# Two slots for product weights and two for condition units in the ring of the convolution part

## The chip, the cores and the metric

One core of one Trainium2 chip. The metric is the device time of the kernel in microseconds (us); less is better. TensorE, VectorE, ScalarE and GpSimd are called PE, DVE, ACT and POOL; SP is the queue that issues most of the loads. PEld is PE's weight load.

## The reference, cut to what matters

One step of a decoder layer on 512 prompt rows and 8 x 8 sample rows (576 columns in all), all in float32. What the change touches is the convolution branch and the condition product that runs beside it:

```python
m = jnp.dot(jax.nn.silu(c), w_ada) + b_ada          # 9 condition rows, 2048 x 12288
h = _rmsnorm(x, norm1) * (1 + sc1) + sh1
z = jnp.dot(h, w_in)                                # 2048 x 4688, za and zg 1024 wide each
a = za * jax.nn.sigmoid(zg)
y = _dwconv_valid(a_hist, w_dw_a, b_dw_a)           # 31 taps along the sequence, 1024 channels
conv_o = jax.nn.silu(_group_layernorm(y, gn_g, gn_b))   # 8 groups of 128 channels
```

The last 30 rows of `a` (and the sample's) are outputs too. After this come the attention part, the merge and a gated MLP.

## The kernel before, in words

The program is written by hand for each engine, with semaphores between them; the order of each engine's instructions is the order of the code. All big products are float32 by three passes: ACT copies a weight tile `raw` to `whi` (`hi`, L735), POOL subtracts, `wlo = raw - whi` in four instructions of 128x256 (`lo`, L663), and PE multiplies `whi` by the high part of the operand, `whi` by its low part, and `wlo` by the high part (`unit`, L1074). `raw` has four slots of 512 KB, `whi` and `wlo` two each.

The convolution part is `mix(i)` for i = 0 to 7, one group of 128 channels each. Two kinds of tiles pass through `raw`:

- four halves of product weights (two of `zg`, two of `za`), which go through ACT and POOL and are then one `part` of 48 matmuls on PE;
- eight condition units (256 x 512 of `w_ada`), which PE reads straight from `raw` (`ada_unit`, L1108), without ACT and POOL. Two of them stand behind each part: a pair.

In the code before, units are numbered 0 to 11 within `mix(i)`: product weights are k = 0, 3, 6, 9, the others condition units, and `Tally.slot` gives slot k mod 4 (plus the base). So each load takes the slot of the unit four places earlier. A load by SP waits until that slot is read: `taken(n)` waits for POOL's subtraction of product weight n (s_lo), `multiplied(n)` for PE's condition unit n (s_au). The loads of product weights k = 6, 9 and 0 of the next group stand in slots of condition units, and wait for these:

```python
ada_done(1)
half(u, 6, 0, win, i * 128 + C_ZA)
...
ada_done(3)
half(u, 9, 1, win, i * 128 + C_ZA)
```

PE in `mix(i)`: part 0, `ada_sum`, `group_var(i-2)` (L1269), pair 0, part 1, `last_rows(i-1)` (L1297), `group_root(i-2)` (L1276), pair 1, part 2, pair 2, `state_in(i)` (L1305), part 3, pair 3, `group_center(i-1)` (L1262). Parts are counted 0 to 3 here in both kernels.

ACT in `mix(i)`: copy of weight 1, `ada_sums`, `squares`, `silu_conv`, copy of weight 2, `ada_out`, `root_var(i-2)` (L813, two small square roots and a table load), copy of weight 3, the sigmoid of zg (`sg`, L851), `last_rows(i-1)` (copies to `cvs`, L825, L826), copy of the next group's weight 0, `state_in`.

DVE in `mix(i)`: the gated product (`hist`, L1830), which waits for part 3 and the sigmoid; then 31 taps in two chains (`yb` L1860, `ye` L1863), with between them the sample rows (`prod` L1844, its reduction L1847), the reciprocal of the roots (L1812) after tap 13, `norm_group` (L1817) after tap 25, the sum of the two chains (L1866), and one step of the top-k of the scores (`take_prompt`, L1795, L1800). DVE's `mix(i)` runs while PE is in `mix(i+1)`.

POOL: the four subtractions of the group, then two output DMAs (L677).

The next part (`U_QKV`) uses the ring of four for product weights alone; there the DVE work of `mix(7)` and eight more top-k steps come first.

Of the kernel before, what the change touches and what calls it, by code (L numbers as in the profile page):

```python
# [114 lines left out]
class Tally:  # L115
# [5 lines left out]
    def __init__(self, base, i=0, per=0):  # L121
        self.base, self.i, self.per = base, i, per
        self.whole = ADA1 if base < U_QKV else ADA1 + ADA2 if base < U_ADB else ADA1 + ADA2 + ADA3
        self.whole_per = 8 if U_MIX <= base < U_QKV else 0

    def slot(self, k, n):
        assert self.per % n == 0
        return (self.base + k) % n

    def turn(self, k, n):  # L130

        return (self.base + k) // n + self.i * (self.per // n)

    def index(self, k):
        if self.whole_per:
            assert k % 3 == 0
            return self.base - self.whole + k // 3 + self.i * (self.per - self.whole_per)
        return self.base - self.whole + k + self.i * self.per

# [35 lines left out]
def layer_program(nc, x_prompt, x_sample, cache_k, cache_v, cache_kidx, state_conv, state_ffn, page_table,  # L175
# [7 lines left out]
    with ctx:  # L183
# [244 lines left out]
        def _(sp):  # L428
            def taken(n):

                sp.wait_ge(s_lo, n + 1)

            def multiplied(n):

                sp.wait_ge(s_au, n + 1)
# [61 lines left out]
            def ada_part(u, k, m, nb):  # L497
                weight(u, k, rows(w_ada[0, m * 256:m * 256 + 256, nb * 512:nb * 512 + 512], 2), 512)

            def mix(i):  # L500
                u = Tally(U_MIX, i, 12)
                ada_done = lambda m: multiplied(ADA1 + 8 * i + m)
                if i == 0:
                    before = [lambda k=k: taken(u.index(0) - 4 + k) for k in range(4)]
                else:
                    before = [lambda: ada_done(-3), lambda: taken(u.index(0) - 1), lambda: ada_done(-2), lambda: ada_done(-1)]
                before[0]()
                half(u, 0, 0, win, i * 128 + C_ZG)
                before[1]()
                ada_part(u, 1, 0, i + 8)  # L510
                before[2]()
                ada_part(u, 2, 1, i + 8)
                before[3]()
                half(u, 3, 1, win, i * 128 + C_ZG)
                w(sp, s_stt, i)
                sp.dma_start(stN[:, :, :], state_conv[0].rearrange("b r c -> (b r) c")[:, i * 128:i * 128 + 128]
                             .rearrange("(h p) c -> p h c", h=2)).then_inc(s_stn, 16)
# [6 lines left out]
                taken(u.index(3))  # L524
                ada_part(u, 7, 4, i + 8)
                ada_done(2)
                ada_part(u, 8, 5, i + 8)
                ada_done(3)
                half(u, 9, 1, win, i * 128 + C_ZA)
                taken(u.index(6))  # L530
                ada_part(u, 10, 6, i + 8)
                ada_done(4)
                ada_part(u, 11, 7, i + 8)
            w(sp, s_scD, 1)
            for i in range(8):
                mix(i)

# [13 lines left out]
            n = ADA1 + ADA2  # L551
            before = [lambda: multiplied(n - 3), lambda: taken(u.index(0) - 1), lambda: multiplied(n - 2), lambda: multiplied(n - 1)]
            for c in range(4):
# [101 lines left out]
        def _(pool):  # L655
# [23 lines left out]
            for i in range(8):  # L679
                for k in (0, 3, 6, 9):  # L680
                    lo(Tally(U_MIX, i, 12), k, 1)
                if i:
                    conv_rows(i - 1)
# [18 lines left out]
        def _(act):  # L702
# [131 lines left out]
            def mix(i):  # L834
                u = Tally(U_MIX, i, 12)
                hi(u, 3)
                if i:
# [3 lines left out]
                if i >= 3:  # L841
                    silu_conv(i - 3)
                hi(u, 6)
# [213 lines left out]
        def _(pe):  # L1057
# [250 lines left out]
            def mix(i):  # L1308
# [6 lines left out]
                if i >= 2:  # L1315
                    group_var(i - 2)
                ada_unit(u, 1, 0)
                ada_unit(u, 1, 1)
                part(u, 3, 0, 1)
                if i:  # L1320
# [3 lines left out]
                for m in (2, 3):  # L1324
                    ada_unit(u, 2, m)
                w(pe, s_a, i)
                part(u, 6, 1, 0)
                for m in (4, 5):
                    ada_unit(u, 3, m)
                state_in(i)  # L1330
                part(u, 9, 1, 1)
                for m in (6, 7):
# [305 lines left out]
        def _(dve):  # L1638
# [186 lines left out]
            def mix(i):  # L1825
                u = Tally(U_MIX, i, 12)
                dve.wait_ge(s_used, u.index(9) + 3)
                dve.wait_ge(s_sg, i + 1)
# [344 lines left out]
```

## Time and profile before

| | us |
|---|---|
| median of 3 runs | 3378.21 (3371.06 to 3380.23) |
| the profiled execution, its time | 3379.13 |
| its span in the trace | 3377.5 |
| convolution part, first to last `hist` (seven intervals) | 474.55 to 784.75 |

The trace is of one execution. The starts of `hist` (L1830) on DVE mark the groups: 474.55, 522.69, 566.47, 609.58, 651.83, 696.00, 739.24 and 784.75 us. Every rate below is read between two of these.

### The profile page before, as it was taken

Reading aid. Unit: us, or ns where it says so; the run is one execution under the profiler, and the core shown is the slowest. Engines: PE = TensorE matmul, PEld = TensorE weight load, DVE = VectorE, ACT = ScalarE, POOL = GpSimd, SP = SyncE. Lnnn points to the kernel's source line nnn. Section 1 sums busy time; section 2 is a strip of 40 time slices with the busy share of each in tenths; the row PEclk is TensorE's granted clock in tenths of the full one; section 3 lists DMA queues with packets and bytes.
Section 4 is the critical chain, followed back from the end, with each engine's and each line's share of the span. In section 5 each row is a group of like instructions: output and inputs, shape, how many; then the busy total and the mean of one; then the engine's idle time right before and its main releaser. Section 6 shows DMA issues by size and latency. Waiting matters only on the chain.

```text
span 3377.5 us, 56831 instructions
## 1 busy us (share of the span) xinstructions
PE 3108.6 (92%) x21589; PEld 2767.3 (82%) x21592; DVE 1358.1 (40%) x2796; ACT 899.0 (27%) x1640; POOL 1220.4 (36%) x1694
## 2 busy tenths in 40 slices
PE   6698969899997788799799999999999999999998
PEld 3196357778973444599699999999999999999998
DVE  1524246778877744300523232332323232332322
ACT  2212312323212221211232323232332323232323
POOL 0042333334330023144244444444444444444443
PEclk9897889999998777799699999999999999999999
DMA  7821144553237455423122222322222222222223
GB/s 244 261 73 34 38 140 142 154 154 102 70 110 245 144 152 154 121 75 89 32 82 87 84 82 86 86 82 83 88 83 82 86 85 83 83 86 85 82 84 94
DMA packets 448315, 356.83 MB, mean 106 GB/s; under 512 B 27785, under 2 KB 391973, under 8 KB 446885
## 3 DMA queue, kind: packets, MB, share of 16 engines
q1 hardware_dynamic: 437282, 327.85, 32.6%
q0 software_dynamic: 8704, 19.27, 2.0%
q10 hardware_dynamic: 2075, 6.34, 0.6%
q8 instruction: 158, 2.59, 0.3%
q14 instruction: 96, 0.78, 0.1%
HBM read 346.15 MB, written 7.96 MB: 105 GB/s over the span
## 4 chain that ended last, share of the span: by engine, by line
PE 69%; issue 14%; DVE 5%; POOL 4%; DMA 4%; ACT 2%; SPq 1%; POOLq 0%; DVEq 0%; ACTq 0%
PE ps L1074 58%; POOL wlo L663 4%; DMA raw<-in_w_in 3%; PE ps L1108 1%; PE ps L1214 1%; PE ps L1485 1%; PE ps L1246 1%; PE ps L1472 1%; PE ps L1276 1%; PE ps L1238 1%; DMA raw<-in_w_ada 1%; ACT whi L735 1%; PE ps L1269 1%; PE ps L1435 0%; DVE mx L1964 0%
## 5 line engine op out<-in xcount | busy, mean ns | idle before, releaser
L663 POOL TENSOR_TENSOR wlo<-raw,whi 128x256 fp32r<-128x256 f32 x1480 | 1108.0, 779 | 1715.6 <-ACT whi L735 1715.6
L1074 PE MATMUL ps<-XH,whi 128*128 128x288 f32 (+1 forms) x4512 | 991.0, 301 | 71.8 <-POOL wlo L663 52.5
L1074 PE MATMUL ps<-XH,wlo 128*128 128x288 f32 (+1 forms) x4512 | 977.0, 298 | 0.0
L1074 PE MATMUL ps<-XL,whi 128*128 128x288 f32 (+1 forms) x4512 | 973.1, 297 | 0.0
L735 ACT ACTIVATE whi<-raw 128x1024 fp32r<-128x1024 f32 x370 | 391.2, 1058 | 1744.8 <-PE ps L1074 1463.3
L1074 PEld LDWEIGHTS ps<-XH,whi 128*128 128x128 f32 (+1 forms) x4512 | 734.5, 191 | 100.4 <-issue 47.6
L1074 PEld LDWEIGHTS ps<-XL,whi 128*128 128x128 f32 (+1 forms) x4512 | 734.5, 191 | 0.0
L1074 PEld LDWEIGHTS ps<-XH,wlo 128*128 128x128 f32 (+1 forms) x4512 | 732.0, 191 | 0.0
L2083 DVE SCALAR_TENSOR_TENSOR tmp<-up,vT,tmp 128x512 f32<-128x512 f32 x88 | 98.7, 1121 | 741.4 <-ACT tmp L972 739.0
L1074 PE MATMUL ps<-gH,whi 128*128 128x288 f32 x1408 | 301.6, 295 | 2.5 <-ACT us L965 2.0
L1074 PE MATMUL ps<-gH,wlo 128*128 128x288 f32 x1408 | 302.3, 296 | 0.0
L1074 PE MATMUL ps<-gL,whi 128*128 128x288 f32 x1408 | 299.2, 294 | 0.0
L2052 DVE TENSOR_TENSOR yS<-ps,adaT 128x64 f32<-128x64 f32 x192 | 43.1, 224 | 596.8 <-PE ps L1074 595.5
L1074 PEld LDWEIGHTS ps<-gH,whi 128*128 128x128 f32 x1408 | 225.6, 188 | 3.2 <-ACT us L965 2.2
L1074 PEld LDWEIGHTS ps<-gL,whi 128*128 128x128 f32 x1408 | 225.2, 188 | 0.0
L1074 PEld LDWEIGHTS ps<-gH,wlo 128*128 128x128 f32 x1408 | 224.9, 188 | 0.0
L1108 PE MATMUL ps<-raw,csT 128*32 128x512 f32 x768 | 154.8, 679 | 36.1 <-DMA raw<-in_w_ada 35.8
L418 POOL DMA_DIRECT2D Vp<-in_cache_v x128 | 68.7, 537 | 316.7 <-issue 316.7
L1108 PEld LDWEIGHTS ps<-raw,csT 128*32 128x32 f32 x768 | 22.0, 115 | 109.9 <-DMA raw<-in_w_ada 83.3
L2053 DVE SCALAR_TENSOR_TENSOR x1T<-ps,adaT,x1T 128x288 f32<-128x288 f32 (+1 forms) x192 | 97.6, 508 | 0.0
L1860 DVE SCALAR_TENSOR_TENSOR yb<-hist,vT,yb 128x512 f32<-128x512 f32 x120 | 96.3, 802 | 0.0
L1863 DVE SCALAR_TENSOR_TENSOR ye<-hist,vT,ye 128x512 f32<-128x512 f32 x112 | 89.4, 799 | 0.0
(291 smaller groups left out, 2669.9 us busy)
## 6 DMA issues: line engine op xcount, KB each, us to landing
raw<-in_w_ada SPq DMA_DIRECT2D x192, 512.0 KB, 4.7
raw<-in_w_up SPq DMA_DIRECT2D x176, 512.0 KB, 4.0
raw<-in_w_down SPq DMA_DIRECT2D x88, 512.0 KB, 3.6
raw<-in_w_in SPq DMA_DIRECT2D x72, 512.0 KB, 5.0
Vp<-in_cache_v POOLq DMA_DIRECT2D x128, 128.0 KB, 3.0
raw<-in_w_out SPq DMA_DIRECT2D x32, 512.0 KB, 4.0
Kp<-in_cache_k SPq DMA_DIRECT2D x64, 128.0 KB, 2.7
KpB<-in_cache_k SPq DMA_DIRECT2D x64, 128.0 KB, 2.8
```

Of the source, the lines that this page charges most:

```text
L418: eng.dma_start(dst(k), cache[0, bass.ds(pg, 1)].rearrange("a s g d -> s (a g d)" if len(cache.shape) == 5 else "a s d -> s (a d)")).then_ ...
L663: last = G.tensor_tensor(wlo[:, u.slot(m, 2), a:a + width // 4], raw[:, u.slot(m, 4), a:a + width // 4], whi[:, u.slot(m, 2), a:a + width ...
L735: A.activation(whi[:, u.slot(m, 2), 0:width], raw[:, u.slot(m, 4), 0:width], ACT.Copy)\
L1074: ins = mm(dst[:, t, :], wt, x(k0 + k, t), start=st, stop=sp_)
L1108: ins = mm(ps_all[g:g + 32, bk, :], csT[:, kt, :], raw[:, s, kt % 2 * 512:kt % 2 * 512 + 512], start=kt < 4, stop=kt >= KT - 4)
L1214: mm(bank(6 + n % 2, 128, 0, S), qiT[p:p + 64, h // 2, (j + 1) * 128:(j + 2) * 128], kiT[p:p + 64, 0:S], start=True, stop=True).then_inc(s ...
L1238: mm(bank(SCORE_BANKS[x % 3], 128, 0, 256 if t < 32 else DS), qiD[p:p + 64, b, :, :].rearrange("p c t -> p (c t)"), keys, start=True, stop ...
L1860: STT(even, hist[:, k:k + SEQ], w_tap(i, k), even, ALU.mult, ALU.add).then_inc(s_pe_, 1)
L1863: STT(odd, hist[:, k:k + SEQ], w_tap(i, k), odd, ALU.mult, ALU.add).then_inc(s_po, 1)
L2052: link.hold(TT(by8(yS[:, :]), by8(bank(2 * slot + 1, 128, SEQ - TH, TH)), gs, ALU.mult))
L2053: STT(row[:, 0:TH], a, gp, row[:, 0:TH], ALU.mult, ALU.add)
L2083: link.hold(STT(pa, up[:, v, 1:1 + SEQ], tap(1), pa, ALU.mult, ALU.add))
```

## The change

- Slots: within the convolution part product weights use slots 0 and 1, condition units slots 2 and 3. The four product weights are now k = 0 to 3, the condition units k = 4 to 11. `turn` counts the loads of each slot, and the slots of all later parts are turned by two.
- SP: product weight n + 1 is asked for ahead of the condition pair of weight n, and waits for the subtraction of weight n - 1 (`taken`). The condition unit m waits for unit m - 2 of the same kind (`multiplied`).
- ACT: `last_rows(i - 1)` stands ahead of the sigmoid.
- PE, POOL, DVE: the same instructions in the same order; only the numbers waited for differ.

```diff
     def slot(self, k, n):
         assert self.per % n == 0
-        return (self.base + k) % n
+        if self.mix:
+            return k % 2 if k < 4 else 2 + k % 2
+        return (self.ring + k) % n
...
-            def mix(i):
+            def mix_weight(n):
+
+                i, q = n // 4, n % 4
                 u = Tally(U_MIX, i, 12)
-                ada_done = lambda m: multiplied(ADA1 + 8 * i + m)
...
-                taken(u.index(0))
-                ada_part(u, 4, 2, i + 8)
-                ada_done(0)
-                ada_part(u, 5, 3, i + 8)
-                ada_done(1)
-                half(u, 6, 0, win, i * 128 + C_ZA)
...
+                taken(u.index(q) - 2)
+                half(u, q, q % 2, win, i * 128 + (C_ZG, C_ZA)[q // 2])
+
+            def mix_ada(n):
+
+                i, q = n // 4, n % 4
+                u = Tally(U_MIX, i, 12)
+                for m in (2 * q, 2 * q + 1):
+                    if n:
+                        multiplied(ADA1 + 8 * i + m - 2)
+                    else:
+                        taken(u.index(0) - 4 + m)
+                    ada_part(u, 4 + m, m, i + 8)
             w(sp, s_scD, 1)
-            for i in range(8):
-                mix(i)
+            mix_weight(0)
+            mix_weight(1)
+            mix_ada(0)
+            for n in range(1, 32):
+                if n < 31:
+                    mix_weight(n + 1)
...
+                mix_ada(n)
...
-                hi(u, 9)
-                act.wait_ge(s_used, u.index(3) + 3)
+                hi(u, 3)
+                if i:
+                    last_rows(i - 1)
+                act.wait_ge(s_used, u.index(1) + 3)
                 w(act, s_a, i)
                 A.activation(halves(sg[:, :]), pair(0), ACT.Sigmoid).then_inc(s_sg, 1)
-                if i:
-                    last_rows(i - 1)
```

SP's queue in the middle of the convolution part, before (s_lo is counted by POOL's subtraction, s_au by PE's condition units):

```order
L438 DMA raw<-in_w_ada 128x2x512 [waits s_lo]
L438 DMA raw<-in_w_ada 128x2x512 [waits s_au]
L494 DMA raw<-in_w_in 128x8x128 [waits s_au]
L516 DMA stN<-in_state_conv 120x2x128 [waits s_stt]
L438 DMA raw<-in_w_ada 128x2x512 [waits s_lo]
L438 DMA raw<-in_w_ada 128x2x512 [waits s_au]
L494 DMA raw<-in_w_in 128x8x128 [waits s_au]
```

and the same stretch now:

```order
L500 DMA raw<-in_w_in 128x8x128 [waits s_lo]
L533 DMA stN<-in_state_conv 120x2x128 [waits s_stt]
L444 DMA raw<-in_w_ada 128x2x512 [waits s_au] x2
L500 DMA raw<-in_w_in 128x8x128 [waits s_lo]
L444 DMA raw<-in_w_ada 128x2x512 [waits s_au] x2
L500 DMA raw<-in_w_in 128x8x128 [waits s_lo]
```

The load of a product weight (`in_w_in`) waited for a condition unit, and waits for a subtraction now; the condition units wait for condition units alone.

ACT around the sigmoid, before (`cvs` is `last_rows`, s_psample and s_stt belong to `state_in`):

```order
L735 ACTIVATE whi<-raw 128x1024 [waits s_used,s_raw3]
L851 ACT_TABLE_LOAD [waits s_a]
L851 ACTIVATE sg<-ps 128x576 [waits s_used]
L825 ACTIVATE cvs<-ps 64x128 [waits s_ao,s_at]
L826 ACTIVATE cvs<-ps 30x128
L735 ACTIVATE whi<-raw 128x1024 [waits s_used,s_raw2]
L832 ACTIVATE hs<-ps 128x8x30 [waits s_psample,s_stt]
```

and now:

```order
L733 ACTIVATE whi<-raw 128x1024 [waits s_used,s_raw1]
L823 ACTIVATE cvs<-ps 64x128 [waits s_ao,s_at]
L824 ACTIVATE cvs<-ps 30x128
L851 ACT_TABLE_LOAD [waits s_a]
L851 ACTIVATE sg<-ps 128x576 [waits s_used]
L733 ACTIVATE whi<-raw 128x1024 [waits s_used,s_raw0]
L830 ACTIVATE hs<-ps 128x8x30 [waits s_psample,s_stt]
```

The two copies to `cvs` moved past the sigmoid and its table load, and the slots read are 1 and 0 in place of 3 and 2.

## Rows read from the trace of the kernel before

**Rows 1.** The page: busy time and share of the span.

```profile
PE 3108.6 (92%) x21589; PEld 2767.3 (82%) x21592; DVE 1358.1 (40%) x2796; ACT 899.0 (27%) x1640; POOL 1220.4 (36%) x1694
```

**Rows 2.** Windows: PE, PEld, DVE, ACT, POOL busy; clock, DMA share, GB/s last.

```profile
474.55:522.69 48.14, 33.42 (x241) 29.11 (x237) 33.05 (x51) 6.48 (x14) 25.32 (x19) 0.89 0.46 135
...
609.50:651.83 42.33, 37.27 (x265) 31.96 (x269) 34.63 (x53) 12.90 (x23) 14.60 (x18) 0.96 0.53 154
```

**Rows 3.** Waits from 440 to 810 us: total us, times, longest us.

```profile
ACT whi L735 <- DMA raw<-in_w_in: 255.4, 32, 18.9
...
DVE hist L1830 <- issue: 44.7, 7, 14.9
...
PE ps L1074 <- POOL wlo L663: 28.4, 11, 11.6
DVE rs L1812 <- ACT rs L814: 27.1, 6, 5.2
```

**Rows 4.** Chain that ended last, around the group of 609.5: start us, us.

```profile
610.48 1.06 PE ps L1262 x2
611.70 6.40 PE ps L1074 x48
618.10 0.79 PE ps L1116 x8
618.89 1.24 PE ps L1269 x10
620.13 1.07 PE ps L1108 x8
...
621.56 5.06 DMA raw<-in_w_in
...
643.82 7.92 PE ps L1074 x48
```

**Rows 5.** The same chain: the part's beginning, and a part at full clock.

```profile
439.02 7.90 PE ps L1074 x48
...
525.63 6.59 PE ps L1074 x48
```

**Rows 6.** DVE in order of time in one group: start, us, [idle before].

```profile
651.83 0.46 DVE L1830 TENSOR_TENSOR hist<-ps,sg 128x288 f32<-128x288 f32 x1 [3.68 <-issue]
...
655.16 4.01 DVE L1844 TENSOR_TENSOR prod<-hs,vT 128x1984 f32<-128x1984 f32 x1
```

**Rows 7.** DVE in order of time: a tap alone, and one under POOL's subtraction.

```profile
639.04 0.74 DVE L1860 SCALAR_TENSOR_TENSOR yb<-hist,vT,yb 128x512 f32<-128x512 f32 x1
639.70 1.22 DVE L1863 SCALAR_TENSOR_TENSOR ye<-hist,vT,ye 128x512 f32<-128x512 f32 x1
```

**Rows 8.** POOL in order of time: two whole subtractions, four instructions each.

```profile
436.11 2.76 POOL L663 TENSOR_TENSOR wlo<-raw,whi 128x256 fp32r<-128x256 f32 x4 [20.72 <-ACT whi L735]
...
482.29 4.59 POOL L663 TENSOR_TENSOR wlo<-raw,whi 128x256 fp32r<-128x256 f32 x4 [4.94 <-ACT whi L735]
```

**Rows 9.** POOL in the window 492 to 496: one instruction of the next subtraction.

```profile
492.68 11.41 POOL L663 TENSOR_TENSOR wlo<-raw,whi 128x256 fp32r<-128x256 f32 x1 [5.79 <-ACT whi L735]
```

**Rows 10.** POOL in order of time after the last `hist` at 784.75.

```profile
785.88 3.63 POOL L663 TENSOR_TENSOR wlo<-raw,whi 128x256 fp32r<-128x256 f32 x4 [3.22 <-ACT whi L735]
794.51 3.27 POOL L663 TENSOR_TENSOR wlo<-raw,whi 128x256 fp32r<-128x256 f32 x4 [5.00 <-ACT whi L735]
```

**Rows 11.** DVE after the last `hist`: the step that rows 6 end with.

```profile
789.98 3.97 DVE L1844 TENSOR_TENSOR prod<-hs,vT 128x1984 f32<-128x1984 f32 x1
```

**Rows 12.** Loads of condition units by SP (L438), 480 to 780 us.

```profile
DMA to landing us min/median/max: 3.6/3.9/7.3
```

**Rows 13.** The chain after the last `hist`, to the last reciprocal of the roots.

```profile
784.75 0.46 DVE hist L1830
...
795.78 2.13 DVE yb L1847
...
851.43 0.20 DVE rs L1812
```

More of the change, by code:

```diff
@@ L123, in __init__ @@
         self.whole = ADA1 if base < U_QKV else ADA1 + ADA2 if base < U_ADB else ADA1 + ADA2 + ADA3
-        self.whole_per = 8 if U_MIX <= base < U_QKV else 0
+        self.mix = U_MIX <= base < U_QKV
+        self.ring = base + (2 if base >= U_QKV else 0)
     def slot(self, k, n):
         assert self.per % n == 0
-        return (self.base + k) % n
+        if self.mix:
+            return k % 2 if k < 4 else 2 + k % 2
+        return (self.ring + k) % n
     def turn(self, k, n):
-        return (self.base + k) // n + self.i * (self.per // n)
+        if self.mix:
+            s = self.slot(k, n)
+            before = (U_MIX + 3 - s) // 4
+            return before + (2 * self.i + k // 2 if k < 4 else 4 * self.i + (k - 4) // 2)
+        late = (-8 if (self.ring + k) % n < 2 else 7) if self.base >= U_QKV else 0
+        return (self.ring + k) // n + self.i * (self.per // n) + late
     def index(self, k):
[L135 to L138, printed above, removed]
+        assert not self.mix or k < 4
+        return self.base - self.whole + k + self.i * (self.per - 8 if self.mix else self.per)
 class Chain:
@@ L498, in ada_part @@
                 weight(u, k, rows(w_ada[0, m * 256:m * 256 + 256, nb * 512:nb * 512 + 512], 2), 512)
-            def mix(i):
+            def mix_weight(n):
+                i, q = n // 4, n % 4
                 u = Tally(U_MIX, i, 12)
-                ada_done = lambda m: multiplied(ADA1 + 8 * i + m)
[L503 to L517, printed above, removed]
-                taken(u.index(0))
-                ada_part(u, 4, 2, i + 8)
-                ada_done(0)
-                ada_part(u, 5, 3, i + 8)
-                ada_done(1)
-                half(u, 6, 0, win, i * 128 + C_ZA)
[L524 to L533, printed above, removed]
@@ new lines, in _ @@
+            w(sp, s_scD, 1)
+            mix_weight(0)
[4 more added lines that the diff above has]
+                    mix_weight(n + 1)
+                if n % 4 == 1:
+                    i = n // 4
+                    w(sp, s_stt, i)
+                    sp.dma_start(stN[:, :, :], state_conv[0].rearrange("b r c -> (b r) c")[:, i * 128:i * 128 + 128]
+                                 .rearrange("(h p) c -> p h c", h=2)).then_inc(s_stn, 16)
+                mix_ada(n)
@@ L551, in _ @@
             n = ADA1 + ADA2
-            before = [lambda: multiplied(n - 3), lambda: taken(u.index(0) - 1), lambda: multiplied(n - 2), lambda: multiplied(n - 1)]
+            before = [lambda: taken(u.index(0) - 2), lambda: taken(u.index(0) - 1), lambda: multiplied(n - 2), lambda: multiplied(n - 1)]
             for c in range(4):
@@ L679, in _ @@
             for i in range(8):
-                for k in (0, 3, 6, 9):
-                    lo(Tally(U_MIX, i, 12), k, 1)
+                lo(Tally(U_MIX, i, 12), 0, 4)
                 if i:
@@ L835, in mix @@
                 u = Tally(U_MIX, i, 12)
-                hi(u, 3)
+                hi(u, 1)
                 if i:
@@ L842, in mix @@
                     silu_conv(i - 3)
-                hi(u, 6)
+                hi(u, 2)
                 if i:
@@ L1316, in mix @@
                     group_var(i - 2)
-                ada_unit(u, 1, 0)
-                ada_unit(u, 1, 1)
-                part(u, 3, 0, 1)
+                for m in (0, 1):
+                    ada_unit(u, 4, m)
+                part(u, 1, 0, 1)
                 if i:
@@ L1324, in mix @@
                 for m in (2, 3):
-                    ada_unit(u, 2, m)
+                    ada_unit(u, 4, m)
                 w(pe, s_a, i)
-                part(u, 6, 1, 0)
+                part(u, 2, 1, 0)
                 for m in (4, 5):
-                    ada_unit(u, 3, m)
+                    ada_unit(u, 4, m)
                 state_in(i)
-                part(u, 9, 1, 1)
+                part(u, 3, 1, 1)
                 for m in (6, 7):
```

2 lines of the change are left out of this document (1 added, 1 removed).

## The prediction

> **What bounds the kernel now.** I read the page first, then the windows between the starts of `hist`, the waits of the convolution part, the chain that ended last, and last DVE and POOL in order of time. The page says that PE is busy in 92% of the span [rows 1], so the gain can only come from stretches where it is not. The convolution part is one: in a group of 42.33 us PE is busy for 37.27 and DVE for 34.63 [rows 2]. Neither is full, so something goes back and forth between them.
>
> The chain shows what. Pair 0 on PE (620.13) is followed at once by the load of product weight 2 (621.56, 5.06 us), then ACT, then POOL; the same happens after the next pair [rows 4]. The load stands in a slot that the pair has only just left, and costs about 5 us each time, with ACT's copy and POOL's subtraction behind it. In the waits it is the first line: ACT waited 255.4 us, in 32 waits, for product weights [rows 3]. ACT's order is fixed, so what stands behind its late copy is late too: the roots, for which DVE's reciprocal waits 27.1 us over 6 groups, and the sigmoid. PE waits directly for POOL 28.4 us in 11 waits, and `hist` on DVE waits 44.7 us over seven groups [rows 3]. A part that comes after such a wait is also slow: 7.92 us against 6.40 [rows 4] and 6.59 [rows 5], with the granted clock at 0.89 to 0.96 of 2.4 GHz over the groups [rows 2].
>
> From the first `hist` (474.55) to the last (784.75) go 310.2 us, 44.3 a group. After the last one the chain is DVE's own for 66.7 us, to the reciprocal at 851.43 [rows 13], and then PE's. So the time of the last `hist` decides: what it moves, the end moves.
>
> **The loads.** The product weight n + 1 now waits for the subtraction of weight n - 1, and stands behind the condition pair of n - 1, which waits for pair n - 2. Both are done when part n - 1 starts. So it is asked for a whole part and a pair before ACT can use it (ACT's copy then waits for part n - 1 to leave `whi`): 5.06 us of load [rows 4] against a part of 6.6 [rows 5]. The 255.4 us of waits turn into waits for PE, which cost nothing while copy (1.1, as from `hist` to POOL's start after the last group [rows 10, 13]) and subtraction (2.8 to 4.6 [rows 8, 10]) fit under the next part.
>
> The condition units lose room: a pair is asked for only when the pair before has been multiplied. Between the two stands at least one part, 6.6 us, and the load takes 3.9 (at most 7.3) [rows 12], plus 0.36 of SP's issue (from the pair's end at 621.20 to 621.56 [rows 4]). I take 0; if each of the two tightest pairs of a group had the 7.3, they would cost 2 x 1.1 = 2.2 us a group, which is the upper bound. Below zero it can't be, as nothing waits for these loads now. SP issues three loads where it issued three: the queue has no more work, and the state rows' load (`stN`) still waits for an earlier group only. The move of `last_rows` puts two copies of a quarter microsecond ahead of the sigmoid; `hist` needs the sigmoid only after part 3, so I cost it at nothing; its cover is parts 2 and 3. It frees PE's `state_in`. POOL's output DMAs stay behind the fourth subtraction, and their data comes earlier.
>
> **PE's floor.** In the group of 42.33 us PE is busy for 37.27 [rows 2], with one slow part in it (7.92 for 6.59, [rows 4, 5]). Without it 37.27 - 1.33 = **35.9 us**.
>
> **DVE's floor.** `hist` to `hist` from 609.58 to 651.83 is 42.25 us. Of this 3.68 is the wait for part 3 [rows 6], and one in six of the 27.1, say 3.8, the wait for the roots [rows 3]: 34.8 left. In it are taps that ran against POOL: a tap alone takes 0.74, one against a subtraction 1.22 [rows 7], and there were five: 5 x 0.48 = 2.4. That leaves **32.4 us** for DVE alone.
>
> **Where POOL and DVE meet.** This is what the change moves most. POOL was let in mostly while DVE waited; DVE will hardly wait. Counting from the end of part 3 as 0:
> - Subtraction of weight 1, asked at 1.1: this is the situation after the last `hist`, where POOL started 1.13 us after it [rows 10, 13]. `prod` came 5.24 us after `hist` there, and 3.33 in rows 6 [rows 6, 11]: DVE loses 1.9.
> - Weight 2: pair 3, centre, part 0 end at 1.07 + 1.2 + 6.4 = 8.7, the copy at 9.7. Again as after the last `hist` (794.51, 9.8 after it, 3.27 us, [rows 10]): it goes in at the reduction of `prod`, DVE loses 0.5.
> - Weight 3: part 1 ends at 8.7 + 0.79 + 1.24 + 1.07 + 6.6 = 18.4 [rows 4, 5], the copy at 19.5. DVE's reciprocal then is past: 3.3 to `prod` and 4.0 for it [rows 6], 2.1 for the reduction [rows 13], ten taps of 0.66 (from 639.04 to 639.70 [rows 7]) and 0.2 are 16.2, and the 2.4 lost make 18.6. Then 12 taps of 0.66 run without a gap until `norm_group` at about 26.6. A run of taps shuts POOL out: one instruction that needs 2.76 / 4 = 0.69 [rows 8] took 11.41 us [rows 9], until the run ended. So this subtraction goes in at 26.6 and is done at about 30.2. Part 3 could start at 35.9 - 6.6 = 29.3: PE waits 0.9. DVE loses 3 x 0.48 = 1.5.
> - The next group's weight 0 comes right behind, DVE loses another 1.5; PE needs it only after pair 3 and the centre.
>
> Together DVE takes 32.4 + 1.9 + 0.5 + 1.5 + 1.5 = 37.8, PE 35.9 + 0.9 = 36.8. When DVE falls behind PE, the first subtraction falls on the top-k step and on `hist` and costs less, about 1 of its 1.9. So I take **37.0 us a group**, with 35.9 and 37.8 as the near ends.
>
> The Trainium skill (SBUF — State Buffer, section on the two separate sides) says that VectorE and GpSimd share a port pair as an exclusive lock, held for a whole instruction, by a VectorE operation with two SBUF inputs too, and that whoever starts first has it. By that rule, the trace agrees on POOL's side (11.41 us [rows 9]). On DVE's side the rows show a loss of 0.48 a tap where the rule, taken by its words, would make it POOL's whole instruction; I take the row, and price the rule as rival 4.
>
> **First groups.** To the first `hist`: parts 2 and 3 no longer wait for loads asked for after pairs 0 and 1. After part 0 (439.0 to 446.9) come three parts, one at perhaps 7.5 us, three pairs and `state_in`: 446.9 + 1.1 + 7.5 + 1.1 + 6.6 + 1.1 + 0.4 + 6.6 = 471.3, so 3.3 earlier. The first interval (48.14 before, with the blocked subtraction in it [rows 2, 9]) has no reciprocal and no `norm_group` on DVE. PE has no variance and roots there either, so the subtraction for part 3 is asked at about 17, while DVE's taps run through to about 30; it is done at 33, part 3 at 39.6. I take **39.7**.
>
> **The sum.** The last `hist` comes at 471.3 + 39.7 + 6 x 37.0 = 733.0, against 784.75: 51.8 us earlier. What follows is the same work. 3379.1 (the profiled execution; its span is 3377.5) - 51.8 = 3327.3. The median of the runs is 0.9 lower than the profiled time, so I forecast **3326 us**. A measurement of this kernel tells about 0.3%, 10 us, from no change.
>
> **Rivals.**
> 1. *POOL waits longer.* If `norm_group` (one operand in SBUF) doesn't let POOL in, weight 3 waits for the end of the taps, near 31; it is done at 34.5, part 3 at 41.2, and the next group follows: 41.2 a group. For it: 11.41 us [rows 9]. Against: 4.59 us at 482.29 went in at a reduction in mid-run [rows 8]. Last `hist` at 471.3 + 7 x 41.2 = 759.7, gain 25: 3353. Chance 0.13.
> 2. *DVE pays for every subtraction.* If all 16 instructions of a group meet taps, 16 x 0.48 = 7.7 and DVE takes 40.1 a group: last `hist` at 752, gain 33: 3345. For it: DVE has no idle time left in which they could fall. Against: the reduction, the top-k step and `hist` are in every group and are no taps. Chance 0.13.
> 3. *The condition pairs come late.* 35.9 + 2.2 = 38.1, and parts behind such waits slow down (+1.3 each, twice): 40.7, gain 28: 3350. For it: 7.3 us has occurred [rows 12]; against: the median is 3.9. Chance 0.05.
> 4. *No change.* Each of the 16 POOL instructions of a group holds DVE up for its whole 0.69 us [rows 8]: 32.4 + 11.0 = 43.4 us a group, last `hist` at 775.1, gain 9.7: 3369. For it: POOL is wholly shut out while a tap runs [rows 9], and the reverse could hold. Against: taps under a subtraction took 1.22, not 0.74 + 0.69 [rows 7]. Chance 0.03. (It is the page's rule above, taken by its words.)
> 5. *Slower.* One mechanism: POOL's subtraction of weight 2, asked at 9.7, misses the reduction and every other gap and goes in only when the taps end, near 31. Then part 2 starts at 34.3, part 3 follows at 42.4 and ends at 49: 49 a group, last `hist` at 814, 29 us late: 3408. It is slower from (784.75 - 471.3) / 7 = 44.8 us a group on. For it: rows 9. Against: the same step let POOL in twice [rows 8, 10]. Chance 0.04.
>
> My forecast, 35.9 to 38.5 a group (3316 to 3336), has 0.62. **Range:** 3313 (every group at PE's floor) to 3350, which takes in rival 2 and half of 3; about 0.2 is left out. **Faster** by over 0.3%: 0.62 + 0.13 + 0.13 + 0.05 = 0.93; **same** 0.03; **slower** 0.04.
>
> **What would show it.** Starts of `hist` 36 to 38 us apart; ACT's wait for product weights near zero, its waits for PE up; the wait of the reciprocal for the roots gone; DVE busy in over 90% of a group; parts at 6.4 to 6.6; one subtraction a group that takes 7 us or more. Intervals of 40 and more with PE waiting for POOL would speak for rival 1, with taps at 1.2 throughout for rival 2, with PE waiting for `in_w_ada` for rival 3. If `hist` comes 50 us earlier but the end doesn't, the 66.7 us behind it were not DVE's alone.

## The result, and the profile after

| | before | after |
|---|---|---|
| median of 4 runs, us | 3374.64 (3370.87 to 3380.23) | 3326.89 (3319.95 to 3327.74) |
| ratio | | 0.9861, 95% interval 0.9843 to 0.9879 |
| span of the profiled execution, us | 3377.5 | 3325.7 |
| first and last `hist`, us | 474.55 and 784.75 | 470.11 and 735.19 |

The change is 47.8 us faster by the medians; the profiled executions are 51.8 apart. Line numbers of the kernel after are 2 lower on most engines (L1072 is the product, L662 POOL's subtraction, L733 ACT's copy, L1828 `hist`, L500 and L444 the loads).

The page, busy time of each engine. PE is busy for 26 us less than in [rows 1], and DVE and POOL for 16 and 26 us more, though their instructions are the same:

```profile
PE 3082.3 (93%) x21589; PEld 2745.4 (83%) x21592; DVE 1374.0 (41%) x2796; ACT 899.8 (27%) x1640; POOL 1246.4 (37%) x1694
```

Windows between starts of `hist`, columns as in [rows 2] (PE, PEld, DVE, ACT, POOL busy, then clock, DMA share, GB/s):

```profile
587.33:624.06 36.73, 35.42 (x263) 30.51 (x262) 36.55 (x54) 12.42 (x24) 16.70 (x18) 1.00 0.59 177
624.06:661.82 37.76, 35.42 (x249) 30.85 (x251) 36.00 (x54) 11.54 (x22) 16.76 (x18) 0.91 0.55 169
```

The group shown takes 36.73 us where the one of [rows 2] took 42.33, and in it DVE is now busy for 36.55. The second row is a group in which PE had to wait and then ran at a clock of 0.91. The stretch from the second to the last `hist` (six groups), after and before:

```profile
512.24:735.19 222.95, 217.38 (x1574) 186.27 (x1566) 220.28 (x318) 74.75 (x134) 103.73 (x104) 0.98 0.58 174
```
```profile
522.69:784.75 262.06, 234.07 (x1570) 198.95 (x1566) 204.34 (x319) 75.23 (x138) 89.86 (x112) 0.92 0.51 149
```

A group takes 37.2 us in the mean, where it took 43.7. DVE does the same instructions in 16 us more. POOL's windows don't hold the same work: the one after has 104 instructions and the one before 112, two subtractions more, and POOL is still busy for 14 us longer in the one after. That is the price of meeting each other. DVE is busy for 220.28 of 222.95 us. PE needs 16.7 us less, since its parts run at a clock of 0.98 and not 0.92.

The waits from 440 to 760 us, as in [rows 3]:

```profile
ACT whi L733 <- DMA raw<-in_w_in: 146.5, 22, 15.6
ACT whi L733 <- PE ps L1072: 75.8, 11, 12.9
...
DVE hist L1828 <- issue: 9.5, 2, 7.9
...
PE ps L1072 <- POOL wlo L662: 15.1, 3, 8.6
...
DVE rs L1810 <- ACT rs L812: 4.2, 1, 4.2
```

`hist` waited 44.7 us and waits 9.5, nearly all of it in the first interval; the reciprocal waited 27.1 us and waits once. ACT still stands idle for 146.5 us until loads land, which I had not expected. That is all the idle time that a load ended, most of it time in which ACT had nothing to do, so it isn't a cost by itself; e7 tests that. DVE in order of time, the second and the fourth `hist`: 7.94 us of idle time ahead of the one, none ahead of the other:

```profile
512.24 0.46 DVE L1828 TENSOR_TENSOR hist<-ps,sg 128x288 f32<-128x288 f32 x1 [7.94 <-issue]
```
```profile
587.33 0.46 DVE L1828 TENSOR_TENSOR hist<-ps,sg 128x288 f32<-128x288 f32 x1
```

DVE's taps in the middle of a group (the reciprocal at 604.19), and POOL's subtractions there, both in order of time:

```profile
605.58 0.74 DVE L1858 SCALAR_TENSOR_TENSOR yb<-hist,vT,yb 128x512 f32<-128x512 f32 x1
606.24 1.22 DVE L1861 SCALAR_TENSOR_TENSOR ye<-hist,vT,ye 128x512 f32<-128x512 f32 x1
...
609.67 1.22 DVE L1858 SCALAR_TENSOR_TENSOR yb<-hist,vT,yb 128x512 f32<-128x512 f32 x1
610.82 0.74 DVE L1861 SCALAR_TENSOR_TENSOR ye<-hist,vT,ye 128x512 f32<-128x512 f32 x1
```
```profile
490.69 12.44 POOL L662 TENSOR_TENSOR wlo<-raw,whi 128x256 fp32r<-128x256 f32 x4 [5.10 <-ACT whi L733]
...
605.66 4.68 POOL L662 TENSOR_TENSOR wlo<-raw,whi 128x256 fp32r<-128x256 f32 x4 [6.75 <-ACT whi L733]
```

One subtraction holds up four taps by 0.48 us each (606.24 to 609.67). Four instructions of POOL take 4.68 us among taps, and took 12.44 in the first interval, where the first of them alone took 9.94 us: POOL was shut out.

In that interval, the part behind this subtraction. PE's first row of it, and then the window of the whole part, columns as above:

```profile
503.19 0.61 PE L1072 MATMUL ps<-XH,whi 128*128 128x288 f32 x1 [4.25 <-POOL wlo L662]
```
```profile
503.19:512.14 8.95, 8.95 (x52) 8.79 (x56) 1.11 (x3) 0.00 (x0) 3.81 (x6) 0.71 0.23 64
```

PE had stood idle for 4.25 us, and the part took 8.95 us at a clock of 0.71, where a part without such a wait takes 6.6.

Last, the chain that ended last, from the end of the convolution part to the first product of the next one:

```profile
726.56 1.07 PE ps L1106 x8
728.00 1.18 SPq L444
729.23 6.83 DMA raw<-in_w_in
736.08 1.07 ACT whi L733
737.22 7.77 POOL wlo L662 x4
745.13 9.12 PE ps L1072 x48
```

Here the load is back on the chain. The first weight of the next part (L455) is asked for behind the last condition pair, not ahead of it as all weights of the convolution part are. PE was idle for 8.63 us ahead of the product at 745.13, which then took 9.12 us.

A table of where the time went, by marks in both traces (differences of starts, worked out from the rows of `hist`, the last reciprocal of the group roots, and the first product of logits):

| from | to | before | after |
|---|---|---|---|
| start | first `hist` | 474.55 | 470.11 |
| first `hist` | second | 48.14 | 42.13 |
| second `hist` | last, six groups | 262.06 | 222.95 |
| last `hist` | last reciprocal of group roots | 66.7 | 74.1 |
| there | first logits | 146.9 | 142.8 |
| first logits | end | 2379.2 | 2373.6 |

The last row is work that the change doesn't touch. In the profiles of the kernels below it comes out between 2366 and 2376 us, and at 2371 to 2375 in the three that are made from the kernel before (e2, e4, e10), so its 5.6 us are scatter and not a gain.

### The profile page after: what moved, and what is told of

It reads as the page before. It is cut to its first block, busy times and chain, and to the rows that moved or that the text cites. A ratio compares the mean times of both kernels' runs of the same rounds, so it can differ in the third digit from the quotient of the medians.

```text
span 3325.7 us, 56891 instructions
## 1 busy us (share of the span) xinstructions
PE 3082.3 (93%) x21589; PEld 2745.4 (83%) x21592; DVE 1374.0 (41%) x2796; ACT 899.8 (27%) x1640; POOL 1246.4 (37%) x1694
## 4 chain that ended last, share of the span: by engine, by line
PE 70%; issue 13%; DVE 9%; POOL 4%; DMA 1%; ACT 1%; SPq 1%; POOLq 0%; DVEq 0%; ACTq 0%
PE ps L1072 60%; POOL wlo L662 4%; DVE yb L1858 2%; DVE ye L1861 2%; PE ps L1483 1%; PE ps L1212 1%; PE ps L1244 1%; PE ps L1106 1%; DMA raw<-in_w_ada 1%; PE ps L1236 1%; DVE prod L1842 1%; PE ps L1470 1%; PE ps L1274 1%; DMA raw<-in_w_in 1%; PE ps L1433 1%
## 5 line engine op out<-in xcount | busy, mean ns | idle before, releaser
L662 POOL TENSOR_TENSOR wlo<-raw,whi 128x256 fp32r<-128x256 f32 x1480 | 1134.0, 797 | 1636.9 <-ACT whi L733 1636.9
L1072 PE MATMUL ps<-XH,whi 128*128 128x288 f32 (+1 forms) x4512 | 986.4, 299 | 59.3 <-POOL wlo L662 40.0
L1072 PE MATMUL ps<-XH,wlo 128*128 128x288 f32 (+1 forms) x4512 | 972.9, 297 | 0.0
L1072 PE MATMUL ps<-XL,whi 128*128 128x288 f32 (+1 forms) x4512 | 966.3, 296 | 0.0
L733 ACT ACTIVATE whi<-raw 128x1024 fp32r<-128x1024 f32 x370 | 391.1, 1058 | 1699.3 <-PE ps L1072 1526.7
L1072 PEld LDWEIGHTS ps<-XH,whi 128*128 128x128 f32 (+1 forms) x4512 | 729.5, 190 | 84.6 <-issue 45.8
L1072 PEld LDWEIGHTS ps<-XL,whi 128*128 128x128 f32 (+1 forms) x4512 | 729.7, 190 | 0.0
L1072 PEld LDWEIGHTS ps<-XH,wlo 128*128 128x128 f32 (+1 forms) x4512 | 727.0, 189 | 0.0
L1072 PE MATMUL ps<-gH,whi 128*128 128x288 f32 x1408 | 301.9, 295 | 2.5 <-ACT us L963 2.0
L1072 PE MATMUL ps<-gH,wlo 128*128 128x288 f32 x1408 | 302.3, 296 | 0.0
L1072 PE MATMUL ps<-gL,whi 128*128 128x288 f32 x1408 | 298.6, 294 | 0.0
L1072 PEld LDWEIGHTS ps<-gH,whi 128*128 128x128 f32 x1408 | 225.8, 188 | 3.2 <-ACT us L963 2.2
L1072 PEld LDWEIGHTS ps<-gL,whi 128*128 128x128 f32 x1408 | 225.4, 188 | 0.0
L1072 PEld LDWEIGHTS ps<-gH,wlo 128*128 128x128 f32 x1408 | 224.4, 188 | 0.0
L1106 PE MATMUL ps<-raw,csT 128*32 128x512 f32 x768 | 150.6, 661 | 37.4 <-DMA raw<-in_w_ada 37.2
L1858 DVE SCALAR_TENSOR_TENSOR yb<-hist,vT,yb 128x512 f32<-128x512 f32 x120 | 104.7, 873 | 0.0
L1861 DVE SCALAR_TENSOR_TENSOR ye<-hist,vT,ye 128x512 f32<-128x512 f32 x112 | 97.2, 868 | 0.0
```

The lines of the kernel that those rows point to most:

```text
L662: last = G.tensor_tensor(wlo[:, u.slot(m, 2), a:a + width // 4], raw[:, u.slot(m, 4), a:a + width // 4], whi[:, u.slot(m, 2), a:a + width ...
L733: A.activation(whi[:, u.slot(m, 2), 0:width], raw[:, u.slot(m, 4), 0:width], ACT.Copy)\
L1072: ins = mm(dst[:, t, :], wt, x(k0 + k, t), start=st, stop=sp_)
L1106: ins = mm(ps_all[g:g + 32, bk, :], csT[:, kt, :], raw[:, s, kt % 2 * 512:kt % 2 * 512 + 512], start=kt < 4, stop=kt >= KT - 4)
L1858: STT(even, hist[:, k:k + SEQ], w_tap(i, k), even, ALU.mult, ALU.add).then_inc(s_pe_, 1)
L1861: STT(odd, hist[:, k:k + SEQ], w_tap(i, k), odd, ALU.mult, ALU.add).then_inc(s_po, 1)
```

## The experiments

In each, the time is the median of the runs, and the ratio is to the kernel before, run beside it on the same chip, with a 95% interval. The median of the kernel before was 3374.64 us beside the change, 3371.26 beside e1 to e4, 3371.15 beside e5 to e8 and 3368.89 beside e9 to e12, so kernels of different sets are compared by their ratios. "The groups" are the 222.95 us of six groups in the profile.

### Which half of the change

**e1**, the ring without the move of the last rows:

```diff
-                if i:
-                    last_rows(i - 1)
                 act.wait_ge(s_used, u.index(1) + 3)
                 w(act, s_a, i)
                 A.activation(halves(sg[:, :]), pair(0), ACT.Sigmoid).then_inc(s_sg, 1)
+                if i:
+                    last_rows(i - 1)
```

> The change without its move of the last rows: the copies to cvs stand behind the sigmoid again. Theory: the whole gain is the ring's, the move is hidden under parts 2 and 3, so this is the change's own time, 3327 within 5 us, with starts of hist 36 to 38 us apart. Rival (the move matters, as it frees bank 5 for state_in and lets the next copy of weight 0 start earlier): PE waits 1 us or more ahead of state_in in each group, 3334 or more.

Measured: 3325.12 us, ratio 0.9874 (0.9855 to 0.9892). As the theory said: the interval takes in the change's 0.9861. In the profile first and last `hist` are 268.2 us apart, 3.1 more than in the change, with six of the seven intervals between 36.6 and 38.5.

**e2**, the kernel before with the move alone (`last_rows` ahead of the sigmoid):

> The kernel before with the move of the last rows alone. In its trace state_in waited for cvs 6.2 us in six waits, between pair 2 and part 3, where PE then waited for POOL's subtraction anyway. Theory: no change, 3375 within 5 us. Rival (the move is worth what state_in waited): 6 us faster, 3369.

Measured: 3370.94 us, ratio 1.0011 (0.9996 to 1.0026). The move is worth nothing that can be measured. The 6.2 us of waits for `cvs` are gone from the profile, and PE's waits for POOL's subtraction have grown from 28.4 to 37.3 us: the one lay beside the other. The ring carries the gain, as far as these intervals tell.

### Is DVE the bound now?

**e3**, one more MAX8 of 64x2056 behind each of the seven top-k steps:

```diff
                 if i < 7:
                     take_prompt()
+                    V.max(out=mx8[0:NS, 3, :], in_=scD[:, :])
```

> The change, with one MAX8 over scD (2.29 us in the traces) more on DVE behind each of the seven top-k steps of the convolution part. Theory: in groups 2 to 5 and 7 DVE had no idle time ahead of hist, so it is the bound; each of these grows by 2.3 us, together 12 to 16 us: 3339 to 3343. Rival (PE at 35.9 us of work is the bound and DVE only follows): DVE has slack, under 5 us in all: 3327 to 3332.

Measured: 3334.16 us, ratio 0.9893 (0.987 to 0.9916). The theory in kind, not in size. In the profile first and last `hist` are 276.4 us apart in place of 265.1: 11.4 us more, of 16.0 added. The first of the seven was free, as `hist` waited for PE in that interval (41.66 us, 42.13 in the change); the other six, 13.7 us, made the six groups 11.8 us longer. But the reciprocal came 67.9 us after the last `hist` and not 74.1: PE came later to the late load of the next part's weight, and was idle for 3.84 us ahead of that part in place of 8.63. So 7.6 us arrived at the end of the profiled execution (3333.3 against 3325.7). The interval of the ratio touches the change's (0.9870 and 0.9879), so it is the intervals of `hist` that speak against the rival, and not the time.

**e4**, the same line in the kernel before:

> The kernel before with the same seven MAX8. There hist waits at least 3.6 us in each group, more than the 2.29 us, so both theories expect no change: 3375 within 4 us. If it grows by 10 us or more, DVE was a bound before too, in spite of its idle time.

Measured: 3368.18 us, ratio 0.9995 (0.998 to 1.0011). The same 16 us cost nothing there that can be measured, and less than 4 by the interval. DVE had room before and has next to none after.

**e9**, the change without six of the prompt's sixteen top-k steps, which it leaves out:

```diff
-                if i < 7:
+                if i == 0:
                     take_prompt()
```

> The change, with six of the prompt's sixteen top-k steps (those of groups 1 to 6) left out. Each is about 3.3 us on DVE. Theory (DVE at 37 us bounds a group, PE's floor of 35.9 is next): hist comes 36.0 to 36.6 us after the one before in the later groups, the last hist about 5 us earlier, and as DVE then waits 2 us a group the rest of its 3.3 us buys nothing: 3319 to 3323. Rival (a group is as long as DVE's work however short): 3.3 us a group, 20 us: 3307.

Measured: 3317.45 us, ratio 0.9839 (0.9816 to 0.9862). The six groups took 216.50 us, 36.1 each, and `hist` waited for PE again:

```profile
510.15:726.65 216.50, 212.85 (x1568) 182.97 (x1562) 207.16 (x253) 75.14 (x134) 112.86 (x104) 1.00 0.58 178
```

The theory's 36.0 to 36.6 us a group came out, and the rival, 3.3 us a group, did not; the time is 1.6 us below the theory's range. Some 19 us of DVE's work were taken away, DVE's busy time fell by 13.1 only (220.28 to 207.16), and the groups became 6.5 us shorter. PE's floor of about 36 us is right behind: DVE holds a group at 37.2 us, and PE would hold it at 36.1.

### What does POOL cost DVE?

**e8**, two more POOL instructions of 128x256 behind each subtraction, of two SBUF operands:

```diff
                     last.then_inc(s_lo, 1)
+                    if extra is not None:
+                        w(pool, s_px, 2 * (extra + m))
+                        for a in range(2):
+                            G.tensor_tensor(sq[:, 1, a * 256:a * 256 + 256], XH[:, 0, 0:256].bitcast(F32), XH[:, 1, 0:256].bitcast(F32),
+                                            ALU.subtract).then_inc(s_px, 1)
...
-                lo(Tally(U_MIX, i, 12), 0, 4)
+                lo(Tally(U_MIX, i, 12), 0, 4, extra=4 * i)
```

> The change, with two more POOL instructions of 128x256 behind each of the 32 subtractions (of two SBUF operands, into a tile that nobody reads). Eight more a group. Theory (DVE is the bound and pays 0.48 us for each that meets a tap): 2 to 4 us a group more, 12 to 25 us in all: 3339 to 3352. Rival (the lock costs DVE POOL's whole 0.69 us): 5.5 us a group, 38: 3365. Rival (POOL alone waits, and DVE pays nothing): under 5 us, 3327 to 3332.

Measured: 3347.46 us, ratio 0.992 (0.9895 to 0.9945). First and last `hist` were 286.2 us apart, 21.1 more than the 265.1 of the change. For 8 instructions in each of seven intervals that is 0.38 us each, in the length of the intervals. Not all of it is DVE's. In the six groups, 18.9 us longer, DVE is busy for 232.06 us and not 220.28: 11.8 us more, 0.25 for each of 48 instructions added, as if about half of them met a tap. The rest is idle time of DVE. PE waited 16.3 us for the reciprocal from 440 to 760 us, where it waited 5.6 in the change, and its clock over the six groups was 0.92 and not 0.98. POOL alone in order of time, a subtraction and the extra pair behind it, in a run of taps:

```profile
569.98 4.12 POOL L663 TENSOR_TENSOR wlo<-raw,whi 128x256 fp32r<-128x256 f32 x4 [4.54 <-ACT whi L739]
574.06 2.30 POOL L669 TENSOR_TENSOR sq<-XH 128x256 f32<-128x256 f32 x2
```

So the meeting is paid on both sides: POOL's pair takes 2.30 us where it takes 1.44 at 564.00 in the same trace, and DVE pays 0.48 us for each that meets a tap. The price is neither nothing nor POOL's whole instruction, and the forecast of 3339 to 3352 us holds.

### Where POOL is shut out

**e6**, a MEMSET of one element ahead of taps 14 and 22 of the first group:

```diff
                     if k == 14 and i:
                         inverse(0, s_vsq, i)
+                    if k == 14 and i == 0:
+                        bearer()
+                    if k == 22 and i == 0:
+                        bearer()
```

> The change, with a MEMSET of one element ahead of taps 14 and 22 in the first group, whose taps run without a gap (the subtraction at 490.69 took 12.44 us there). Theory: a DVE instruction that reads no two SBUF operands lets POOL in, as the reciprocal does in later groups: no subtraction over 8 us in the first interval of hist, which falls from 42.1 to 38 or 39, 3323. Rival (POOL is let in by the length of a pause and not by the kind of instruction): the interval stays at 42, 3327.

Measured: 3323.8 us, ratio 0.9853 (0.9828 to 0.9878). The first interval fell from 42.13 to 37.60 us, the subtraction there from 12.44 to 4.50. The two before it, 11.71 us together, stayed long, as no MEMSET stands ahead of them. DVE, then POOL, in order of time:

```profile
491.58 0.74 DVE L1862 SCALAR_TENSOR_TENSOR yb<-hist,vT,yb 128x512 f32<-128x512 f32 x1
491.60 0.06 DVE L1788 MEMSET dum<- 128x1 f32 x1
492.24 1.22 DVE L1865 SCALAR_TENSOR_TENSOR ye<-hist,vT,ye 128x512 f32<-128x512 f32 x1
```
```profile
491.85 4.50 POOL L662 TENSOR_TENSOR wlo<-raw,whi 128x256 fp32r<-128x256 f32 x4 [4.22 <-ACT whi L733]
```

Right behind the MEMSET the taps take 1.22: POOL is in. In time, the ratio can't be told from the change's own 0.9861. The same two MEMSETs are in three more kernels below. The first interval is 37.6 to 38.9 us in the four kernels that have them, and in those that don't 41.7 to 44.4 with the new ring and 48.1 to 48.3 with the old.

**e10**, the same in the kernel before:

> The kernel before with the two MEMSETs in the first group's taps. Its subtraction at 492.68 waited 10.7 us there, and PE's part 2 with it. Theory (the same opening as in the change): the first interval of hist falls from 48.1 to 39 or 40, as nothing else there waits on DVE: 8 us faster, 3363. Rival (the load of the weight behind it is as late): under 3 us.

Measured: 3360.99 us, ratio 0.9979 (0.9966 to 0.9991), with medians 7.9 us apart and the first interval of `hist` 38.23 us in place of 48.14. POOL there:

```profile
489.20 4.17 POOL L663 TENSOR_TENSOR wlo<-raw,whi 128x256 fp32r<-128x256 f32 x4 [6.13 <-ACT whi L735]
```

Here the gain stands clear in the ratio. This trace also shows the MEMSET at work: POOL asked at 489.20, 4.0 us into a run of taps, and its first instruction took 0.77 us, with the MEMSET at 489.33. In e11 POOL asked at 488.29, the MEMSET came at 490.30, and the first instruction took 2.66 us, to 490.95. The rival of e6, that the length of a pause lets POOL in, has no pause to point to: the starts of the taps on both sides of these MEMSETs are 0.66 or 0.67 us apart, as in any run of taps (e6: 491.58 and 492.24). In the profile the other six intervals came out 5.5 us longer than in the kernel before (267.6 against 262.1 us), so part of the 9.9 us is given back there; the runs don't say why.

### The loads

**e5**, the first weight of the next part ahead of the last condition pair:

```diff
+                if n == 31:
+                    taken(Tally(U_QKV).index(0) - 2)
+                    half(Tally(U_QKV), 0, 0, win, C_K)
                 mix_ada(n)
...
```

> The change, with the first weight of the next part asked for ahead of the last condition pair, as all weights before it. In the trace of the change PE stood idle for 8.7 us ahead of that part, since the load was asked for at 729.23, behind that pair, and landed at 736.08. Theory: the wait was worth about 3.4 us net, as the reciprocal of the last group came 7.5 us later than in the kernel before (74.1 us after the last hist in place of 66.7) and 4.1 us of this were made good by a PE that no longer waits there: 67 us from the last hist to that reciprocal, 3322 to 3325 against 3327 and 3325. Rival (the wait is on the chain in full): 7 to 8 us, 3319. Rival (DVE's work there hides it): 0.

Measured: 3322.08 us, ratio 0.9858 (0.9833 to 0.9882). The profile shows the mechanism: the reciprocal came 67.8 us after the last `hist`, not 74.1, and PE began the next part's first product at 733.70, with no idle time ahead of it. The forecast of the time lies inside the scatter; the ratio doesn't tell it from the change.

**e7**, every product weight ahead of the pair of its step as well:

```diff
+            mix_weight(2)
             for n in range(1, 32):
-                if n < 31:
-                    mix_weight(n + 1)
+                if n < 30:
+                    mix_weight(n + 2)
+                else:
+                    q = n - 30
+                    taken(Tally(U_QKV).index(q) - 2)
+                    half(Tally(U_QKV), q, q, win, C_K)
...
```

> As the run before last (first weight of the next part early), and every product weight asked for ahead of the condition pair of its step, so one pair and most of a part earlier. In the change ACT still waited 146.5 us for these loads, each landing about 1 us after part n - 1 had left whi. Theory: these waits have 8 us of cover (copy and subtraction fit under the next part), DVE is the bound: within 3 us of the run with the first weight early. Rival (ACT's late copy is on the chain through POOL's place among the taps): 1 us a group, 8 us faster.

Measured: 3319.45 us, ratio 0.9841 (0.9815 to 0.9868). The waits of ACT from 440 to 760 us became

```profile
ACT whi L738 <- PE ps L1077: 209.3, 34, 16.1
```

with no row of ACT for loads any more, and first and last `hist` are 266.8 us apart, as in e5 (266.8). So the 146.5 us of waits for loads in the change cost the groups nothing. The time is within the 3 us of e5 that the theory gave.

### Together

**e11**, e7 and e6 in one:

> The change with all weights asked for ahead of the pairs (the next part's first two too) and the two MEMSETs. Theory: the first weight's 3 to 4 us and the gap's 4 us add up: 3317 to 3320. Rival (what the gap wins is lost by the time DVE bounds the later groups): as with the loads alone, 3321.

Measured: 3316.39 us, ratio 0.9844 (0.9824 to 0.9863). First and last `hist` are 260.1 us apart, where e7 had 266.8, and the reciprocal comes 65.4 us behind. So the profile shows the theory, the gap's gain on top of the loads'; the ratio is e7's 0.9841 and doesn't show it.

**e12**, and five top-k steps moved from the groups to products c = 7 to 11 of the next part:

```diff
-                if i < 7:
+                if i in (0, 3):
                     take_prompt()
...
-                if c < 7:
+                if c < 12:
                     take_prompt()
-                elif c < 12:
+                if 7 <= c < 12:
                     take_sample()
```

> The run before, with five of the prompt's top-k steps moved out of the convolution part (those of groups 1, 2, 4, 5 and 6) to the products c = 7 to 11 of the next part, where DVE was busy 13.1 to 14.0 us in each 16 to 17. All is computed. Theory: as DVE bounds the groups and PE the products, the groups fall to 36.0 to 36.6 us and the products stay: 4 to 6 us faster than the run before, 3313. Rival (3.3 us more do not fit there, as DVE's steps there stand ahead of what PE waits for): 5 us or more slower than the run before.

Measured: 3312.28 us (3300.93 to 3315.94), ratio 0.9815 (0.9795 to 0.9835). This is the fastest kernel of the study; its interval lies below that of the change, while it overlaps e11's at the edge. The six groups took 214.51 us, 35.75 each (the theory had 36.0 to 36.6), against 36.9 in e11. From the reciprocal to the logits it took 148.2 us where e11 took 145.4, so 2.8 of the 6.7 us won in the groups were given back in the products.

## Why the prediction was right, point by point

The forecast was 3326 us, and the median 3326.89. The agreement within 1 us is luck. From the profiles: the last `hist` came 2.2 us later than forecast (735.19, forecast 733.0), the reciprocal behind it another 7.4 late, 4.1 of that came back before the logits, and 5.6 us of scatter in the untouched rest made up for what was left. The gain by the medians is 47.8 us, and the forecast had 51.8, from a kernel before that is 3.6 us slower by its first three runs (3378.21) than by its four (3374.64).

- **The mechanism.** Right. The loads are off the chain of the groups, the roots, `hist` and PE no longer wait for them, and the parts run at the higher clock. e1 and e2 show that it is the ring, and that the move of the last rows costs and brings nothing that can be measured, as I had it.
- **37.0 us a group.** Measured 222.95 / 6 = 37.2. The parts of the sum were less good. I had the third subtraction shut out until `norm_group`; it was let in within 0.6 us in the group shown (605.66 to 606.24), and took 4.68 us. So it met four taps and not three, and PE didn't wait for it. In none of the change's six groups was the third subtraction shut out; in e1, e3, e6, e7, e9 and e12 it was, in one group each and in e9 in two, for 6.5 to 6.7 us and until `norm_group`, as I had it. DVE's own sum does come out: 32.4 for DVE alone, and nine taps under POOL in the group of 587.33 (one at 598.36 and eight of 1.14 or so in two runs), 9 x 0.48 = 4.3, are 36.7, and 36.73 was measured.
- **DVE as the bound, PE close behind.** Right: e3 against e4, and e9 for the floor of PE (36.1 us a group where I had 35.9).
- **The first interval.** I had 39.7, it was 42.1. "Done at 33" came out: the subtraction ended at 503.13, 33.0 us after `hist`. It was asked for at 20.6 and not 17, as the subtraction of weight 1, at 472.91, had been held up too (8.56 us) and the part behind it took 7.95; but the end of the taps set when it was let in. The step that failed is the next one, "part 3 at 39.6": I gave the part 6.6 us, and after 4.25 us without work it took 8.95 (503.19 to 512.14, clock 0.71). [rows 4, 5] had shown 7.92 for parts behind such a wait.
- **The first `hist`.** I had 471.3, it was 470.11: part 0 took 9.11 us and not 7.9, but the three parts behind it took 6.55 each, and I had one of them at 7.5.
- **"What follows is the same work".** This step failed. The last `hist` came at 735.19 (I had 733.0), but then the reciprocal took 74.1 us and not 66.7. I had read the edit as SP's order within the convolution part, and not seen that the next part's first load stays behind the last pair, where its slot is free a pair earlier. e5 moves it and gets 67.8. Of the 7.4 us lost, 4.1 came back before the logits, for which I see a reason in the two chains: before, PE waited for the reciprocal and then ran a product of 8.36 us, and after, PE came later and its product took 6.55. No run isolates that.
- **ACT's wait "near zero".** Wrong: 146.5 us. I counted 5.06 us for a load; behind two condition units it lands after 6.2 us in the median and 7.6 at most, about as long as a part. e7 shows that this costs nothing, since copy and subtraction have the whole next part for cover.
- **The condition pairs.** They cost 0, as taken; no wait of PE for `in_w_ada` is in the waits. Landing took 4.5 us in the median, 6.4 at most.
- **The range.** Its lower end, 3313, is called every group at PE's floor. By the terms of the prediction that floor gives 471.3 + 7 x 35.9 = 722.6 for the last `hist`, 62.2 us earlier, and 3316. The time lies inside either way.
- **The rivals.** Rival 1 (shut out to the end of the taps) happened in the first interval, and in no group. The long pair of subtractions at 664.23 (10.91 us for eight instructions) is another case: one instruction of it took 4.51 us, beside the 4.54 of `prod`. Rival 2 would have been 40.1 us a group; about nine of 16 instructions met taps. Rival 3 had PE waiting for `in_w_ada`, and in the change it never did. Rival 4, the rule of the Trainium skill's page "SBUF — State Buffer" (section on the two separate sides) taken by its words, would have added POOL's 0.69 us each to DVE; each tap that is met costs 0.48, and in e8 DVE's busy time grew by 0.25 for each instruction added. On POOL's side the prediction says that the trace agrees with that rule. The rule speaks of one instruction of VectorE, which is 0.74 us for a tap; the 11.41 us of [rows 9] are 16 taps long, so the rule alone doesn't give them. Rival 5 needed POOL to miss the reduction in every group; the intervals of 35 to 42 us rule that out.

## What to carry to other kernels

A ring of buffers that two kinds of tiles share ties them together: a load waits for the last reader of a slot, whichever kind that was. Giving each kind its own slots took the load off the chain without a byte more of memory. Ask then which engine becomes full, and what it will meet when it no longer pauses: here DVE and POOL had met mostly in DVE's idle time, and of some 55 us of DVE's idle time that the change took out of six groups, 16 came back as busy time beside POOL. And follow the new order past the end of the loop: the first load of the next part kept its old place, and PE stood idle for 8.6 us (what that is worth in time, e5's ratio doesn't tell).

## What the runs showed of the hardware that I had not expected

- A run of taps can keep one POOL instruction out for over 10 us (11.41 in [rows 9], 9.94 within the 12.44 above), but it doesn't always. The first instruction of a subtraction, asked for in a run of taps in two traces, the change's and e9's:

```profile
682.29 0.85 POOL L662 TENSOR_TENSOR wlo<-raw,whi 128x256 fp32r<-128x256 f32 x1 [7.15 <-ACT whi L733]
```
```profile
639.01 6.66 POOL L662 TENSOR_TENSOR wlo<-raw,whi 128x256 fp32r<-128x256 f32 x1 [7.57 <-ACT whi L733]
```

  The one was asked for 1.88 us behind the start of the reciprocal (680.41), the other 2.04 us behind it (636.97). The fourteen traces of this study have 95 such cases in the convolution part, with POOL idle before and at least four taps still to come. In 78, POOL asked at most 1.88 us behind the start of DVE's last instruction of another kind (reciprocal, `norm_group`, MEMSET or another short one), and its first instruction was done in 1.35 us or less. In the other 17 it asked 2.04 us or more behind it, and in 16 of them its first instruction took 6.5 to 13.9 us, to the end of the run (the exception is at 502.80 in e8). So an early request gets in and a late one doesn't. This is what the traces have in common, for taps alone; no run tested it, and why it is so is open. `prod` shut POOL out at 472.91 though POOL asked 1.18 us behind another kind.
- A MEMSET of one element in each partition, 0.06 us, was enough to let POOL in, with the change's ring and with the old one.
- Once POOL is in, the two take turns, at 1.14 us for a tap and a POOL instruction, where one after the other at 0.66 and 0.69 would be 1.35.
- A short idle time of PE costs more than itself. A part takes 6.55 us when PE comes to it without a wait. After 2.18 us without work it took 7.95 (at 481.52, clock 0.81), after 4.25 us 8.95 (503.19, clock 0.71), and after 8.63 us 9.12 (745.13). After a wait of 2.34 us for the reciprocal (at 642.16) the part at 646.71 took 7.30.
